# Feed-forward products of a two-layer decode step: five TensorE products for a weight block instead of six

## The chip, the cores and the metric

The kernel runs on one NeuronCore of a Trainium2 chip. The metric is the device time of one execution in microseconds (us). TensorE (PE in the rows) multiplies, with PEld for its weight loads; VectorE (DVE), ScalarE (ACT), GpSimd (POOL) and SyncE (SP) work beside it, each through its own instruction list, in order.

## The reference

Two layers over 512 prompt tokens and 8 sample tokens (T = 520 columns), model width 1024. Layer 0 mixes with an mLSTM, layer 1 with sliding-window attention. Each layer then runs the feed-forward part that this change touches, and a gated per-layer embedding:

```
u = xn @ w_up                              # 1024 -> 2 x 2816
c = conv_b + sum_j up[:, j:j+T] * conv_w[j]  # 3 taps along the tokens
h = silu(c[..., :2816]) * c[..., 2816:]
y = h @ w_down                             # 2816 -> 1024
```

All products are wanted in nearly full float32 precision.

## The kernel before, in words

Features lie on the 128 partitions and tokens along the free axis. Every operand x is split in two float32r parts, high and low (`xH`, `xL`; `hidH`, `hidL`; `wH`, `wL`), and a product is xH·wH + xL·wH + xH·wL, added up in PSUM. A result has 520 columns, more than the 512 of a PSUM bank, so that each of the three is made for two halves of 260 tokens: six products (`product`, L1173) for a weight block of 128 x 128, each with its own weight load.

The work goes by chunks, and a chunk is 128 output rows. In stage `up0` or `up1` there are 44 chunks of 8 weight blocks (48 products), even ones for the gate side and odd ones for the value side. In `down0` or `down1` there are 8 output tiles of two chunks with 11 blocks each (66 products); the last tile is done by halves in another function (`half_product`) and does not change. The first three up chunks (`SPLIT = 3`) also go by halves and do not change.

Two PSUM tiles of two banks each take the results of successive chunks in turn. Chunk c may begin when the tile of chunk c-2 has been read (`free_after`) and when its low weights are ready (`weights_ready`, the semaphore `s_low`).

In the up stages the other engines work on chunk c in this order, each engine's list written out by hand:

- SP loads the raw weights of chunk c+2 when chunk c-1 is done.
- ACT makes the high weights of chunk c+2 (`high`, L756). Then, for an odd c, it applies Silu to the gate side of c-1 (L971), which has to wait until DVE has ended the convolution of c-1 (L2270). For an even c it does a tiny copy (`touch`, L962) and the high half of the hidden tile (`hid_high`, L963), which has to wait for DVE's gating product of c-1 (L2276). Last of all comes the first tap of the convolution (L977), which waits for DVE's read of c.
- DVE waits for the chunk, reads the PSUM tile and scales it by the norm (`scaled_read`, L1880), makes the low weights of chunk c+2 (`low`, L1832), and does the rest of the convolution (L2262, L2264, L2265, L2270). For an even c the low half of the hidden tile of the pair before (L2280) is among it, for an odd c the gating product (L2276) ends it.

In the down stages a hidden tile has to be whole, high and low, before its block is used: the second chunk of the first output tile waits for the last of the 22 (`s_hid`). ACT copies the result out (L990) and squares it (L993), and DVE adds the squares (L2302).

Of the kernel before, what the change touches and what calls it, by code (L numbers as in the profile page):

```python
# [13 lines left out]
P = 128  # L14
# [4 lines left out]
HT = T // 2  # L19
NL = 2  # L20
# [9 lines left out]
FT = 22  # L30
# [32 lines left out]
for _s in ORDER:  # L63
    CHUNK0[_s] = _c
    for _k in range(COUNT[_s]):
# [13 lines left out]
        _c += 1  # L79

# [57 lines left out]
def build(nc, g):  # L138
    with ExitStack() as ctx:
# [29 lines left out]
        xH = sb("xH", [P, KT, T], F32R)  # L169
        xL_at = sb.top  # L170
        xL = sb("xL", [P, KT, T], F32R)
# [35 lines left out]
        eye = const[:, C_EYE:C_EYE + DEC * DEC]  # L207
        low_at = sb.top
        gate_more = at("gate_more", [P, 2, T], sb.top)
        sg = [u[:, r, 2:2 + T] for r in range(2)] + [gate_more[:, r, :] for r in range(2)]  # L210
        pH = sb("pH", [P, EKT, T], F32R)
        pin_at = sb.top
        pL = sb("pL", [P, EKT, T], F32R)
        pin = at("pin", [P, EKT, T], pin_at)
        arena = sb.top
# [4 lines left out]
        hidH = ff("hidH", [P, FT, T], F32R)  # L220
        hidL = ff("hidL", [P, FT, T], F32R)
# [6 lines left out]
        pxH = em("pxH", [P, KT, T], F32R)  # L228
        pxL = em("pxL", [P, KT, T], F32R)
# [122 lines left out]
        s_psq = sem("ple_square")  # L352
        s_out, s_ystored = sem("stored"), sem("y_stored")
# [48 lines left out]
        def depth(c):  # L402

            return next(DEPTHK[s] for s in reversed(ORDER) if CHUNK0[s] <= c)

# [88 lines left out]
        def _(sp):  # L494
# [54 lines left out]
        def band_and_sinks(pool):  # L549
            made = Chain(pool, s_made)  # L550
            pool.wait_ge(s_const_rest, 16)
# [69 lines left out]
        def _(pool):  # L621
# [81 lines left out]
            for layer in range(NL):  # L703
# [22 lines left out]
                if layer == 0:  # L726
                    pool.wait_ge(s_mm, CHUNK0["ple0"] + 1 + NEXTRA)
# [20 lines left out]
        def _(act):  # L748
# [31 lines left out]
            def inputs(stage, k, q, layer, norm):  # L780
# [4 lines left out]
                nc.scalar.activation(square(stage, q, k), h[:, k, tokens(q)], ACT.Square).then_inc(s_sq, 1)  # L785

# [54 lines left out]
            for c in range(COUNT["kv"]):  # L841
# [11 lines left out]
                if c == 8:  # L853
                    act.wait_ge(s_dml, 1)
                    nc.scalar.activation(wcol[:], wcol[:], ACT.Exp).then_inc(s_wcol, 1)
            def outer_product(b):
# [37 lines left out]
            for c in range(COUNT["qo"]):  # L894
# [7 lines left out]
                if c == 11:  # L902
                    sigmoids(4, 7)

# [11 lines left out]
            def feed_forward(layer, mixer, y, beside):  # L916
# [48 lines left out]
                for c in range(UP):  # L965
# [15 lines left out]
                for c in range(COUNT[down] - 2):  # L981
# [4 lines left out]
                    if c % 2:  # L986
                        k = c // 2
                        act.wait_ge(s_mm, CHUNK0[down] + c + 1)
                        src = bank(down, k)[:, :, 0:HT]
                        nc.scalar.activation(halves(y_down[:, k, :]), src, ACT.Copy)  # L990
                        if k >= 2:
                            act.wait_ge(s_acc, ACC0[down] + k)
                        nc.scalar.activation(halves(sq[:, k % 2, :]), src, ACT.Square).then_inc(s_yr, 1)  # L993
# [52 lines left out]
                def sigmoid(c):  # L1046

                    act.wait_ge(s_read, READ0[ple] + c + 1)
# [93 lines left out]
            for c in range(COUNT["qkv"]):  # L1142
# [8 lines left out]
                if 2 <= c < LASTQ:  # L1151
                    rotate(c)
                if c == 0:
                    act.wait_ge(s_ss, SUM["qkv", 0])
                    nc.scalar.activation(halves(rstd[:]), sums[:, :, 0:HT], ACT.Sqrt, bias=eps[:, 0:1],
                                         scale=1.0 / D).then_inc(s_root, 1)
            exps(BESIDE)
# [14 lines left out]
        def _(pe):  # L1172
            def product(c, w, x, k, out, first, last):  # L1173

                wh, wl = (t[SLOT[c]][:, w * P:w * P + P] for t in (wH, wL))
                for q in range(2):
                    nc.tensor.matmul(out[:, q, 0:HT], wh, x[0][:, k, tokens(q)], start=first, stop=False)  # L1177
                for q in range(2):
                    nc.tensor.matmul(out[:, q, 0:HT], wh, x[1][:, k, tokens(q)], start=False, stop=False)  # L1179
                for q in range(2):  # L1180
                    mm = nc.tensor.matmul(out[:, q, 0:HT], wl, x[0][:, k, tokens(q)], start=False, stop=last)  # L1181
                return mm

            def half_product(c, w, x, k, q, out, first, last):

                wh, wl = (t[SLOT[c]][:, w * P:w * P + P] for t in (wH, wL))
                nc.tensor.matmul(out, wh, x[0][:, k, tokens(q)], start=first, stop=False)  # L1187
                nc.tensor.matmul(out, wh, x[1][:, k, tokens(q)], start=False, stop=False)  # L1188
                return nc.tensor.matmul(out, wl, x[0][:, k, tokens(q)], start=False, stop=last)  # L1189
# [4 lines left out]
            def chunk(stage, k0, x, fresh=False, between=lambda k: None):  # L1194
# [4 lines left out]
                for k in range(KT):  # L1199
                    if fresh:  # L1200
                        pe.wait_ge(s_xr, XSET[stage] + k + 1)
                    mm = product(c, k, x, k, out, k == 0, k == KT - 1)
# [54 lines left out]
            X = (xH, xL)  # L1257
# [43 lines left out]
            def first_chunk(c, k0, k1):  # L1301

                for k in range(k0, k1):
                    if c == 0:
                        pe.wait_ge(s_xr, k + 1)
                    mm = product(c, k, X, k, bank("kv", c), k == 0, k == KT - 1)
# [206 lines left out]
            def feed_forward(layer, mixer, beside):  # L1513
# [30 lines left out]
                d0, hid = CHUNK0[down], (hidH, hidL)  # L1544
                for k0 in range(KT - 1):
                    for part in range(2):
# [9 lines left out]
                        for k in range(DKH):  # L1556
                            mm = product(c, k, hid, part * DKH + k, bank(down, k0), k == 0 and part == 0,
                                         k == DKH - 1 and part == 1)
# [19 lines left out]
                for j in range(KT):  # L1578
# [3 lines left out]
                    for q in range(2):  # L1582
                        if j >= 2:
                            pe.wait_ge(s_pwr, 2 * KT * layer + 2 * (j - 2) + q + 1)
                        for k in range(EKT):
                            mm = half_product(c, EKT * jj + k, (pH, pL), k, q, p_bank(j)[:, q, 0:HT], k == 0, k == EKT - 1)
# [159 lines left out]
            def first_chunks():  # L1746

                def tiles(c, k0, k1):
                    for k in range(k0, k1):
                        pe.wait_ge(s_xr, XSET["qkv"] + k + 1)  # L1750
                        mm = product(CHUNK0["qkv"] + c, k, (pxH, pxL), k, bank("qkv", c), k == 0, k == KT - 1)
# [18 lines left out]
            for c in range(2, COUNT["qkv"]):  # L1770
# [19 lines left out]
                chunk("qkv", c, (pxH, pxL), between=attend)  # L1790
# [33 lines left out]
        def _(dve):  # L1824
# [52 lines left out]
            def scaled_read(stage, c, dst, rows=P, scale=1.0):  # L1877

                dve.wait_ge(s_mm, CHUNK0[stage] + c + 1)
                nc.vector.scalar_tensor_tensor(out=halves(dst), in0=bank(stage, c)[0:rows, :, 0:HT], scalar=scale,  # L1880
                                               in1=halves(rstd[0:rows, :]), op0=ALU.mult, op1=ALU.mult
# [885 lines left out]
```

## Time and profile before

| | us |
|---|---|
| median of 3 runs (1296.8 to 1296.97) | 1296.81 |
| span of the profiled execution | 1294.8 |
| PE busy in it | 1287.4 |
| DVE busy in it | 891.1 |
| ACT busy in it | 594.0 |
| POOL busy in it | 75.0 |

The profiled execution has a span of 1294.8 us, from its first to its last instruction; the timed runs are 2.0 us above that, for what lies around the span. In the rows, L1880 is line 1880 of the kernel before. A timeline row gives the start, the duration, the engine, the line, the operation with the tile written and the tiles read, the shape and the number of instructions merged; in brackets stands idle time before it and what ended it. PEclk is the share of TensorE's full clock (2.4 GHz) that was granted.

### The profile page before, as it was taken

To read this page: it belongs to the slowest core of one execution; us is meant where nothing else is said; L and a number is where in the kernel's file an instruction comes from. 1 tells how busy PE (TensorE), PEld (TensorE's weight loads), DVE (VectorE), ACT (ScalarE), POOL (GpSimd) and SP (SyncE) were. 2 spreads that over 40 slices of the span, in tenths; PEclk is the share of its full clock that TensorE was granted. 3 is DMA by queue.
4 is the path that set the end of the run, shared out by engine and by line. 5 is a ranking of instruction groups with operands and counts; after the bars stand their busy time and mean duration, and the time that the engine had idled before them with its cause. 6 is when DMAs were issued, how large, how long until landed. Compare 5 with 4: busy or idle time off the path is not lost.

```text
span 1294.8 us, 25277 instructions
## 1 busy us (share of the span) xinstructions
PE 1287.4 (99%) x10786; PEld 1254.7 (97%) x10786; DVE 891.1 (69%) x1602; ACT 594.0 (46%) x1060; POOL 75.0 (6%) x117
## 2 busy tenths in 40 slices
PE   9999999999999999999999999999999999999998
PEld 8999989999999999999999978999999999999998
DVE  7899776987777774223897787688777777422385
ACT  6214565544444443223855677554444444222381
POOL 1112230000100000000031020000000000000000
PEclk9999999999999999999999999999999999999999
DMA  5435521213343233222314232311322323322231
GB/s 199 155 100 194 198 99 53 103 58 106 95 105 94 87 111 114 90 90 78 138 59 148 68 97 81 113 52 50 98 94 87 98 84 110 114 90 90 79 130 67
DMA packets 35616, 131.84 MB, mean 102 GB/s; under 512 B 4516, under 2 KB 5260, under 8 KB 35184
## 3 DMA queue, kind: packets, MB, share of 16 engines
q1 hardware_dynamic: 29664, 111.33, 26.8%
q0 software_dynamic: 5408, 18.26, 4.3%
q8 instruction: 85, 1.39, 0.4%
q10 hardware_dynamic: 432, 0.64, 0.2%
q14 instruction: 27, 0.22, 0.1%
HBM read 121.26 MB, written 10.08 MB: 101 GB/s over the span
## 4 chain that ended last, share of the span: by engine, by line
PE 95%; DVE 3%; ACT 1%; DMA 0%; issue 0%; ACTq 0%; DVEq 0%
PE tile L1177 24%; PE tile L1181 24%; PE tile L1179 24%; PE tile L1187 5%; PE tile L1188 5%; PE tile L1189 4%; PE tile L1649 1%; PE side L1187 1%; PE side L1188 1%; PE side L1189 1%; PE sums L1226 0%; DMA raw<-in_w_kv 0%; PE sums L1700 0%; PE sums L1348 0%; PE sums L1707 0%
## 5 line engine op out<-in xcount | busy, mean ns | idle before, releaser
L756 ACT ACTIVATE wH<-raw 128x1024 fp32r<-128x1024 f32 (+1 forms) x190 | 210.9, 1113 | 377.4 <-DMA raw<-in_w_up 145.9
L1177 PE MATMUL tile<-xH,wH 128*128 128x260 f32 x1798 | 362.7, 283 | 0.1
L1181 PE MATMUL tile<-xH,wL 128*128 128x260 f32 x1798 | 362.4, 283 | 0.0
L1179 PE MATMUL tile<-xL,wH 128*128 128x260 f32 x1798 | 361.8, 283 | 0.0
L1832 DVE TENSOR_TENSOR wL<-raw,wH 128x1024 fp32r<-128x1024 f32 (+1 forms) x190 | 245.7, 1294 | 154.5 <-ACT wH L756 150.4
L1177 PEld LDWEIGHTS tile<-xH,wH 128*128 128x128 f32 x1798 | 277.1, 188 | 3.5 <-issue 3.0
L1181 PEld LDWEIGHTS tile<-xH,wL 128*128 128x128 f32 x1798 | 277.2, 188 | 0.0
L1179 PEld LDWEIGHTS tile<-xL,wH 128*128 128x128 f32 x1798 | 276.4, 188 | 0.0
L1880 DVE SCALAR_TENSOR_TENSOR u<-tile,rstd 128x520 f32<-128x520 f32 x96 | 67.2, 700 | 119.5 <-PE tile L1181 119.4
L1177 PE MATMUL tile<-hidH,wH 128*128 128x260 f32 x616 | 124.3, 283 | 0.0
L1181 PE MATMUL tile<-hidH,wL 128*128 128x260 f32 x616 | 123.8, 282 | 0.0
L1179 PE MATMUL tile<-hidL,wH 128*128 128x260 f32 x616 | 123.8, 282 | 0.0
L1187 PE MATMUL tile<-xH,wH 128*128 128x260 f32 x400 | 116.0, 290 | 0.1
L1188 PE MATMUL tile<-xL,wH 128*128 128x260 f32 x400 | 113.1, 283 | 0.0
L1189 PE MATMUL tile<-xH,wL 128*128 128x260 f32 x400 | 112.8, 282 | 0.0
L1179 PEld LDWEIGHTS tile<-hidL,wH 128*128 128x128 f32 x616 | 95.1, 188 | 0.0
L1181 PEld LDWEIGHTS tile<-hidH,wL 128*128 128x128 f32 x616 | 94.9, 188 | 0.0
L1177 PEld LDWEIGHTS tile<-hidH,wH 128*128 128x128 f32 x616 | 94.8, 188 | 0.0
L1187 PEld LDWEIGHTS tile<-xH,wH 128*128 128x128 f32 x400 | 75.3, 188 | 2.8 <-issue 2.3
L1188 PEld LDWEIGHTS tile<-xL,wH 128*128 128x128 f32 x400 | 75.3, 188 | 0.3
L1189 PEld LDWEIGHTS tile<-xH,wL 128*128 128x128 f32 x400 | 75.3, 188 | 0.0
L977 ACT ACTIVATE cv<-u,taps 128x520 f32<-128x520 f32 x44 | 36.2, 824 | 48.2 <-DVE u L1880 47.8
(446 smaller groups left out, 1913.9 us busy)
## 6 DMA issues: line engine op xcount, KB each, us to landing
raw<-in_w_up SPq DMA_DIRECT2D x88, 512.0 KB, 3.6
raw<-in_w_down SPq DMA_DIRECT2D x32, 704.0 KB, 4.1
raw<-in_w_ple SPq DMA_DIRECT2D x16, 512.0 KB, 5.6
raw<-in_w_qo SPq DMA_DIRECT2D x12, 512.0 KB, 3.6
raw<-in_w_qkv SPq DMA_DIRECT2D x12, 512.0 KB, 3.5
raw<-in_w_kv SPq DMA_DIRECT2D x10, 512.0 KB, 3.7
cring<-in_c_in POOLq DMA_DIRECT2D x8, 512.0 KB, 4.8
out_c_s<-cring POOLq DMA_DIRECT2D x8, 512.0 KB, 3.2
```

The lines of the kernel that those rows point to most:

```text
L756: nc.scalar.activation(wH[j][:, 0:n], raw[j][:, 0:n], ACT.Copy).then_inc(s_high, 1)
L977: nc.scalar.activation(dst[:], u[:, r, 2:], ACT.Identity, bias=taps[:, r, 3:4], scale=taps[:, r, 2:3]).then_inc(s_ca, 1)
L1177: nc.tensor.matmul(out[:, q, 0:HT], wh, x[0][:, k, tokens(q)], start=first, stop=False)
L1179: nc.tensor.matmul(out[:, q, 0:HT], wh, x[1][:, k, tokens(q)], start=False, stop=False)
L1181: mm = nc.tensor.matmul(out[:, q, 0:HT], wl, x[0][:, k, tokens(q)], start=False, stop=last)
L1187: nc.tensor.matmul(out, wh, x[0][:, k, tokens(q)], start=first, stop=False)
L1188: nc.tensor.matmul(out, wh, x[1][:, k, tokens(q)], start=False, stop=False)
L1189: return nc.tensor.matmul(out, wl, x[0][:, k, tokens(q)], start=False, stop=last)
L1649: nc.tensor.matmul(banks[half][:, e, at0 + 2 * HD - HD * m + k0:at0 + 3 * HD], queries[r, gp, m * P:m * P + P], qk[r, gp // 2, k0:HD * m + ...
L1832: nc.vector.tensor_tensor(wL[j][:, 0:n], raw[j][:, 0:n], wH[j][:, 0:n].bitcast(F32), ALU.subtract).then_inc(s_low, 1)
L1880: nc.vector.scalar_tensor_tensor(out=halves(dst), in0=bank(stage, c)[0:rows, :, 0:HT], scalar=scale, in1=halves(rstd[0:rows, :]), op0=ALU. ...
```

## The change

For the up chunks from the fourth on and for the down tiles but the last, `wide_product` takes the place of `product`. It splits the tokens in 256 and 264. High and low rows are put beside each other in memory, so that one product of 512 columns makes wH·xH and wH·xL of the first 256 tokens at once, into the two halves of one PSUM bank. wL·xH of those tokens is added to the second half. The other 264 tokens take three products in the second bank, as before.

So the first 256 columns of the result lie in two parts. ACT copies the first part to SBUF (`set_apart`), DVE adds it to the second part in PSUM (`join`), and then 520 columns of the result lie side by side and are read as before. On ACT the copy stands behind Silu or `hid_high` of the same chunk; on DVE the addition stands ahead of the read. The place of the copy in SBUF is that of the constant `band`, which is now loaded on POOL's queue when the last join of layer 0's down stage is done; SP loads the other constants in two pieces, not one.

```diff
+def wide(stage, c):
+    if stage[:2] == "up":
+        return c >= SPLIT
+    return stage[:4] == "down" and c < KT - 1
...
+            def wide_product(c, w, x, k, out, first, last):
+
+                wh, wl = (t[SLOT[c]][:, w * P:w * P + P] for t in (wH, wL))
+                right = out[:, 1, 0:T - WIDE]
+                nc.tensor.matmul(out[:, 0, :], wh, x[:, :, k, 0:WIDE], start=first, stop=last, skip_group_check=True)
+                nc.tensor.matmul(right, wh, x[:, 0, k, WIDE:T], start=first, stop=False)
+                nc.tensor.matmul(right, wh, x[:, 1, k, WIDE:T], start=False, stop=False)
+                nc.tensor.matmul(out[:, 0, WIDE:2 * WIDE], wl, x[:, 0, k, 0:WIDE], start=False, stop=last, skip_group_check=True)
+                return nc.tensor.matmul(right, wl, x[:, 0, k, WIDE:T], start=False, stop=last)
...
+            def set_apart(stage, c):
+                if wide(stage, c):
+                    j = JOIN[stage, c]
+                    act.wait_ge(s_mm, CHUNK0[stage] + (2 * c + 2 if stage[:4] == "down" else c + 1))
+                    if j:
+                        act.wait_ge(s_joined, j)
+                    nc.scalar.activation(apart(stage), bank(stage, c)[:, 0, 0:WIDE], ACT.Copy).then_inc(s_apart, 1)
...
                         hid_high(c // 2 - 1)
+                    set_apart(up, c)
                     act.wait_ge(s_read, READ0[up] + c + 1)
...
+            def join(stage, c):
+                if wide(stage, c):
+                    j, low_results = JOIN[stage, c], bank(stage, c)[:, 0, WIDE:2 * WIDE]
+                    dve.wait_ge(s_apart, j + 1)
+                    nc.vector.tensor_tensor(low_results, low_results, apart(stage), ALU.add).then_inc(s_joined, 1)
...
+                join(stage, c)
                 dve.wait_ge(s_mm, CHUNK0[stage] + c + 1)
+                if wide(stage, c):
+                    dve.wait_ge(s_joined, JOIN[stage, c] + 1)
...
-                        act.wait_ge(s_mm, CHUNK0[down] + c + 1)
-                        src = bank(down, k)[:, :, 0:HT]
+                        set_apart(down, k)
+                        act.wait_ge(s_joined, JOIN[down, k] + 1)
+                        src = results(down, k)
...
                         k = c // 2
+                        join(down, k)
                         dve.wait_ge(s_yr, YREAD0[down] + k + 1)
...
-                        sp.dma_start(const[:, C_CAUSAL:], g.const[:, C_CAUSAL:]).then_inc(s_const_rest, 16)
+                        for piece in (slice(C_CAUSAL, C_BAND), slice(C_SEL, C_ALL)):
+                            sp.dma_start(const[:, piece], g.const[:, piece]).then_inc(s_const_rest, 16)
...
                 if layer == 0:
+                    pool.wait_ge(s_joined, JOIN["down0", KT - 2] + 1)
+                    pool.dma_start(band, g.const[:, C_BAND:C_SEL]).then_inc(s_band, 16)
                     pool.wait_ge(s_mm, CHUNK0["ple0"] + 1 + NEXTRA)
```

## Rows read from the trace of the kernel before

**Rows 1.** The page: span, and the chain of waits by engine.

```profile
span 1294.8 us, 25277 instructions
...
PE 95%; DVE 3%; ACT 1%; DMA 0%; issue 0%; ACTq 0%; DVEq 0%
```

**Rows 2.** Windows (PE, PEld, DVE, ACT, POOL busy; clock; DMA; GB/s): up0, down0, up1.

```profile
256.00:488.00 232.00, 231.96 (x1931) 231.75 (x1930) 172.61 (x331) 101.09 (x144) 5.49 (x5) 1.00 0.32 93
487.00:607.00 120.00, 120.00 (x1000) 120.00 (x1000) 35.82 (x32) 33.32 (x39) 1.10 (x2) 1.00 0.29 96
...
870.00:1102.00 232.00, 231.96 (x1930) 231.75 (x1930) 171.82 (x331) 101.29 (x144) 0.00 (x0) 1.00 0.28 87
```

**Rows 3.** Groups by shape, PEld: one form of weight load (busy us, mean ns).

```profile
L1181 PEld LDWEIGHTS tile<-xH,wL 128*128 128x128 f32 x1798 | 277.2, 188 | 0.0
```

**Rows 4.** Timeline of PE in layer 0's mixer: products of other shapes.

```profile
155.63 1.95 PE L1378 MATMUL tile<-kvq 128*128 128x128 f32 x16
...
172.64 1.03 PE L1400 MATMUL tile<-vtok,prob 128*128 128x257 f32 x4
173.50 0.60 PE L1402 MATMUL tile<-cv,prob 128*128 128x257 f32 x2
```

**Rows 5.** Timeline of DVE, up0: an even chunk, an odd one, the next.

```profile
401.12 0.70 DVE L1880 SCALAR_TENSOR_TENSOR u<-tile,rstd 128x520 f32<-128x520 f32 x1 [1.31 <-PE tile L1181]
401.85 1.22 DVE L1832 TENSOR_TENSOR wL<-raw,wH 128x1024 fp32r<-128x1024 f32 x1
...
404.42 0.74 DVE L2270 SCALAR_TENSOR_TENSOR cg<-u,taps,cg 128x512 f32<-128x512 f32 x1
...
406.88 0.70 DVE L1880 SCALAR_TENSOR_TENSOR u<-tile,rstd 128x520 f32<-128x520 f32 x1 [1.64 <-PE tile L1181]
...
409.70 0.75 DVE L2270 SCALAR_TENSOR_TENSOR cv<-u,taps,cv 128x512 f32<-128x512 f32 x1
410.56 0.70 DVE L2276 TENSOR_TENSOR cv<-cg,cv 128x520 f32<-128x520 f32 x1
...
412.65 0.70 DVE L1880 SCALAR_TENSOR_TENSOR u<-tile,rstd 128x520 f32<-128x520 f32 x1 [1.31 <-PE tile L1181]
```

**Rows 6.** Timeline of ACT in the same chunks.

```profile
405.88 1.06 ACT L756 ACTIVATE wH<-raw 128x1024 fp32r<-128x1024 f32 x1 [3.20 <-DMA raw<-in_w_up]
406.85 0.62 ACT L971 ACTIVATE cg<-cg 128x520 f32<-128x520 f32 x1
```

**Rows 7.** Groups by shape: the nearest kin of copy and addition.

```profile
L801 ACT ACTIVATE y_ml<-tile 128x260 f32<-128x260 f32 x16 | 6.2, 387 | 15.6 <-PE tile L1189 15.5
...
L1888 DVE TENSOR_TENSOR u<-tile,rstd 128x260 f32<-128x260 f32 x8 | 3.1, 423 | 0.1
```

**Rows 8.** Timeline of all engines as chunks 3 and 4 are read.

```profile
261.67 0.69 DVE L1880 SCALAR_TENSOR_TENSOR u<-tile,rstd 128x520 f32<-128x520 f32 x1
261.72 0.64 ACT L971 ACTIVATE cg<-cg 128x520 f32<-128x520 f32 x1 [2.17 <-DVE cg L2270]
...
265.73 0.70 DVE L1880 SCALAR_TENSOR_TENSOR u<-tile,rstd 128x520 f32<-128x520 f32 x1
```

**Rows 9.** Timeline of all engines, chunk 43's read to the second down chunk.

```profile
487.62 0.70 DVE L1880 SCALAR_TENSOR_TENSOR u<-tile,rstd 128x520 f32<-128x520 f32 x1 [1.24 <-PE tile L1181]
488.35 1.62 DVE L1832 TENSOR_TENSOR wL<-raw,wH 128x1408 fp32r<-128x1408 f32 x1
...
491.69 0.70 DVE L2276 TENSOR_TENSOR cv<-cg,cv 128x520 f32<-128x520 f32 x1
492.42 0.20 ACT L962 ACTIVATE touch<-eps 128x1 f32<-128x1 f32 x1 [3.18 <-DVE cv L2276]
492.53 0.62 ACT L963 ACTIVATE hidH<-cv 128x520 fp32r<-128x520 f32 x1
...
493.18 0.70 DVE L2280 TENSOR_TENSOR hidL<-cv,hidH 128x520 fp32r<-128x520 f32 x1 [0.80 <-ACT hidH L963]
...
495.33 0.41 PE L1177 MATMUL tile<-hidH,wH 128*128 128x260 f32 x2
```

More of the change, by code:

```diff
@@ L19 @@
 HT = T // 2
+WIDE = 256
 NL = 2
@@ L79 @@
         _c += 1
+def wide(stage, c):
+    if stage[:2] == "up":
+        return c >= SPLIT
+    return stage[:4] == "down" and c < KT - 1
+JOIN = {}
+for _s in ORDER:
+    for _k in range(KT if _s[:4] == "down" else COUNT[_s]):
+        if wide(_s, _k):
+            JOIN[_s, _k] = len(JOIN)
 READ0, YREAD0, ACC0, SUM, MA0 = {}, {}, {}, {}, {}
@@ L404, in depth, with apart, results, as_results @@
             return next(DEPTHK[s] for s in reversed(ORDER) if CHUNK0[s] <= c)
+        def apart(stage):
+            return apart_late[:] if stage[:3] == "ple" or stage == "qkv" else apart_early
+        def results(stage, c):
+            if wide(stage, c):
+                return bank(stage, c)[:].rearrange("p q t -> p (q t)")[:, WIDE:WIDE + T]
+            return bank(stage, c)[:, :, 0:HT]
+        def as_results(stage, c, ap):
+            return ap if wide(stage, c) else halves(ap)
         def halves(ap):
@@ L1201, in chunk @@
                         pe.wait_ge(s_xr, XSET[stage] + k + 1)
-                    mm = product(c, k, x, k, out, k == 0, k == KT - 1)
+                    mm = (wide_product if wide(stage, k0) else product)(c, k, x, k, out, k == 0, k == KT - 1)
                     if k < KT - 1:
@@ L1305, in first_chunk @@
                         pe.wait_ge(s_xr, k + 1)
-                    mm = product(c, k, X, k, bank("kv", c), k == 0, k == KT - 1)
+                    mm = (wide_product if wide("kv", c) else product)(c, k, X, k, bank("kv", c), k == 0, k == KT - 1)
                 if k1 == KT:
@@ L1542, in feed_forward @@
                     chunk(up, c, X)
-                d0, hid = CHUNK0[down], (hidH, hidL)
+                d0, hid = CHUNK0[down], hidHL
                 for k0 in range(KT - 1):
@@ L1556, in feed_forward @@
                         for k in range(DKH):
-                            mm = product(c, k, hid, part * DKH + k, bank(down, k0), k == 0 and part == 0,
-                                         k == DKH - 1 and part == 1)
+                            mm = wide_product(c, k, hid, part * DKH + k, bank(down, k0), k == 0 and part == 0,
+                                              k == DKH - 1 and part == 1)
                         mm.then_inc(s_mm, 1)
@@ L1750, in tiles @@
                         pe.wait_ge(s_xr, XSET["qkv"] + k + 1)
-                        mm = product(CHUNK0["qkv"] + c, k, (pxH, pxL), k, bank("qkv", c), k == 0, k == KT - 1)
+                        mm = (wide_product if wide("qkv", c) else product)(CHUNK0["qkv"] + c, k, pxHL, k, bank("qkv", c), k == 0, k == KT - 1)
                     if k1 == KT:
@@ L1789, in _ @@
                     pe.wait_ge(s_soft, g)
-                chunk("qkv", c, (pxH, pxL), between=attend)
+                chunk("qkv", c, pxHL, between=attend)
                 if c == 2:
```

63 lines of the change are left out of this document (36 added, 27 removed).

## The prediction, made before the run

> **What bounds the kernel now.** I read the page first: a span of 1294.8 us, and a chain of waits that is PE for 95% of it [rows 1]. Then the windows by stage. In the up stage of layer 0 PE is busy for 231.96 of 232 us with 1931 products, which is 120.1 ns each, at a granted clock of 1.00 (2.4 GHz); in the down stage for 120.00 of 120 us, 1000 products, 120 ns each. Layer 1 repeats layer 0 to the hundredth [rows 2]. DVE is busy for 172.6 of the 232 us and ACT for 101.1. So PE is the bound, and the views that decide are two others: what a product costs apart from its columns, and how long the way is round DVE and ACT from one chunk to the next, because the change adds two steps to that way.
>
> An up chunk is 48 products. Reads of chunks stand at 401.12, 406.88 and 412.65 [rows 5]: 5.765 us a chunk, 11.53 us a pair.
>
> **What PE gains.** At 2.4 GHz 260 columns are 108.3 ns; the product takes 120.1, so 11.8 ns are beside the columns. The block before has 6 x 260 = 1560 columns, the new one 512 + 3 x 264 + 256 = 1560, the same. It has one product less. If the 11.8 ns belong to each product, a block falls from 721 to 709 ns. Bounds, since no float32r product of another width is in the trace: if the excess goes with the columns, the gain is nothing. If instead the weight load paces the products (it is busy for 188 ns at a time, overlapping, and PEld is as full as PE [rows 2, 3]), the four narrow ones stay at 120 ns and the wide one takes its 213.3 ns and 2.5 more. The 2.5 is from a stream of other products: four of 257 columns from 172.64 to 173.50, 215 to 217 ns each, where two passes over 257 columns are 214.2 [rows 4]. That is 696 ns, a gain of 24. A stream with 128 columns and a weight load of the same size goes at about 112 ns ((1.95 - 0.27)/15) [rows 4], so that a load need not take 120 by itself; I take 11.8, between the two.
>
> The row says 120.1 ns for a product of 260 columns. The Trainium skill (TensorE: Matmul & The Clock Gate, Back-to-back issue gap) gives a warm gap of columns / 2.4 + 2.5 ns, which would be 110.8; the trace disagrees. By that rule one product less would save only 2.5 ns a block, and the sum below would end at an estimated 1305.4 us.
>
> Blocks that change: 41 chunks x 8 + 14 x 11 = 482 a layer, 964 in all. If PE set the pace everywhere, the gain would be 964 x 11.8 ns = 11.4 us.
>
> **What the copy and the addition cost.** Nearest kin: an ACT copy of 260 columns from PSUM takes 387 ns, a DVE product of two operands, one in PSUM, 423 ns [rows 7]. For 256 columns I take 0.385 and 0.42 us. DVE's target is PSUM here, which no row shows; at worst I take 0.48, at best 0.38, and for the copy 0.35 to 0.45. Neither step can go into idle time as such, because they lie in a ring. I follow it through, with R for the start of a read and S for the start of the addition.
>
> - S to R: 0.42, and 0.10 for a wait on DVE's own last result behind another wait (the gating product starts at 410.56 where L2270 ended at 410.45 [rows 5]): 0.52.
> - R to the end of the convolution, even chunk: 401.12 to 405.16, 4.04 [rows 5]. Then a crossing to ACT (0.03, as from 492.39 to 492.42 [rows 9]), Silu 0.62, an overlap of 0.09 (406.94 against 406.85 [rows 6]), the copy 0.385, a crossing back 0.03. Even S to odd S: 0.52 + 4.04 + 0.975 = 5.535.
> - R to the end of the gating product, odd chunk: 406.88 to 411.26, 4.38 [rows 5]. Crossing 0.03, `touch` 0.11 until the next starts, the high half 0.62 [rows 9], then -0.09 + 0.385 + 0.03. Odd S to even S: 0.52 + 4.38 + 1.085 = 5.985.
>
> The pair takes 11.52 us. PE alone would take 11.53 - 16 x 0.0118 = 11.34. In the kernel before this ring is open: the read waits for PE alone, and Silu and the high half are done beside PE's next chunk, so that DVE is idle 1.3 to 1.6 us ahead of each read [rows 5]. Now the read waits for the copy, the copy stands behind Silu or `hid_high` on ACT, and these wait for DVE's work on the chunk before. Behind the waiting read on DVE stand the low weights of chunk c+2, and PE waits for those. A lag, once there, can't be made up, for the ring is no faster than PE.
>
> And there is a lag from the start. Chunk 3 is read at 261.67, long after it is done, since DVE and ACT are busy with the first chunks. Silu ends at 262.36 [rows 8]. The copy then ends at 262.66, S(3) = 262.69, R(3) = 263.21. From read 3 to read 4 DVE takes 4.06 us (265.73 - 261.67 [rows 8]), so the gating product ends at 267.27, S(4) = 267.27 + 1.085 = 268.36, R(4) = 268.88: 3.15 us later than before. Chunk 5 starts 1.5 us late (it needs read 3), chunk 6 some 2.6 us late (low weights ready at 268.88 + 0.73 + 1.22 = 270.83). S(5) = 268.88 + 4.04 + 0.975 = 273.90. From there 19 pairs to chunk 43: 273.90 + 19 x 11.52 = 492.78, and 0.40 for the longer low weights in chunk 42 (1.62 against 1.22 [rows 5, 9]): 493.18. R(43) = 493.70, where it was 487.62 [rows 9].
>
> The second down chunk needs the last hidden tile. Before, its low half ended at 493.88, 6.26 us behind R(43), covered by the first down chunk, and PE began at 495.33 [rows 9]. Now it ends at 499.96, and PE begins at 499.99: 4.66 us later, 9.3 us for two layers. Note that PE's own speed doesn't enter into this: up to here the ring sets the time.
>
> Behind that point PE is the bound again. In the down stages DVE is busy for 35.8 and ACT for 33.3 of 120 us [rows 2]; copy and addition lie beside 15.9 us for each tile and cost nothing (without that cover 0.8 us a tile). 13 down chunks a layer, 286 blocks in all, gain 286 x 11.8 ns = 3.4 us. The split load of constants is one DMA issue more on SP early in the first stage, and `band` on POOL's queue is small and awaited much later, by the work on POOL that begins in `ple0`: nothing.
>
> Sum: +9.3 - 3.4 = +5.9 us. The profiled span of 1294.8 would be about 1300.7, the median 1296.8 + 5.9 = **1302.7 us**, slower by 0.45%.
>
> **Rivals.**
> 1. The weight load sets the pace. The ring part stays, down gains 286 x 24 ns = 6.9: +2.4, 1299.2 us. For it speaks that PEld is as full as PE; against it the stream at 112 ns.
> 2. One product less gains next to nothing (the excess goes with the columns): +9.3, 1306.1 us. The rule of the Trainium skill that is cited above would come out near it, at 1305.4 us.
> 3. The other sign: the ring is shorter than I count, and the lag fades. It decides when a pair of chunks takes less than 11.34 us, that is 0.18 less than my sum, 0.09 for each copy and addition, or if Silu and `hid_high` wait less than counted. Then PE is the bound from about chunk 7 on, the two layers lose 2 x 2.6 us at the start and gain 916 x 11.8 ns = 10.8: -5.6, 1291.2 us. For it: each term is small and taken from a neighbour. Against it: all but the addition are seen in this very loop.
> 4. The product of 512 columns, with rows in two runs, goes at half pace, like the 257 columns in 217 ns: a block of some 905 ns, 964 x 184 ns = 177 us more, 1474 us. Nothing speaks for it.
>
> **How the numbers follow.** Chances: forecast 0.50, rival 1 0.20, rival 2 0.15, rival 3 0.12, rival 4 0.03. An error of 0.01 us a chunk in the ring is 39 x 2 x 0.01 = 0.8 us; with copy and addition at their ends (-0.07 and +0.12 a chunk) the sum moves by -5.5 and +9.4, of which I take less than half as likely, 2.5 either way. The range goes from rival 1 less 2.5 to rival 2 and 2.5 more, rounded: 1297 to 1309 us. Within 0.2% (1294.2 to 1299.4 us, what a measurement of this kernel can tell from no change) lies half of rival 1 and little else: 0.13. Slower 0.75, faster 0.12.
>
> **What would show it.** In the profile after: PE idle at chunks 5 and 6, then short waits on the low weights (L1832's successor) every second chunk, the reads spaced by 11.5 us a pair as before; each addition on DVE waiting for ACT, not for PE; a wait of about 2 us for the last hidden tile at the second down chunk; down chunks of 7.80 us where 66 products took 7.93. Wrong at the ring if the reads are spaced by 11.34 or less; wrong at PE if down chunks stay at 7.93 or fall to 7.67.

## The result, and the profile after

The changed kernel takes 1308.17 us (median; 1307.92 to 1308.55), the kernel before in the same session 1296.8 us: a ratio of 1.0089 with an interval of 1.0074 to 1.0103, 11.4 us slower. The forecast was 1302.7, or 5.9 us slower. Its profiled execution spans 1306.3 us against 1294.8 [rows 1], 11.5 us more, at a granted clock of 1.00 in both, so the two profiles can be set against each other.

The page of the kernel after: span, chain of waits by engine, and the group of the new addition.

```profile
span 1306.3 us, 23679 instructions
...
PE 57%; DVE 33%; ACT 6%; issue 4%; DMA 0%; DVEq 0%; ACTq 0%
...
L1943 DVE TENSOR_TENSOR tile<-tile,const 128x256 f32<-128x256 f32 x96 | 42.4, 442 | 95.6 <-ACT const L830 95.6
```

PE is still busy for 99% of the span, but the chain that ended last runs over PE for 57% of it and no longer for 95% [rows 1]; for 39% it goes through DVE and ACT. That is the sign of a ring: PE looks busy, and what sets the time is the way round two other engines. The last row says where: ahead of the 96 additions DVE was idle for 95.6 us, all of it until ACT's copy (L830), none until PE.

The windows of `up0` and `down0` (columns as in [rows 2]):

```profile
255.00:487.00 232.00, 228.75 (x1580) 213.57 (x1579) 185.24 (x360) 109.09 (x179) 5.49 (x5) 1.00 0.30 90
503.00:603.00 100.00, 100.00 (x701) 93.81 (x700) 29.27 (x27) 27.84 (x32) 0.25 (x1) 1.00 0.29 97
```

In the up stage PE is idle for 3.3 us, where it was for 0.04 [rows 2]; in the down stage, from 503 us on, it is never idle. Of the 3.3 us, 2.6 lie where the forecast had them, ahead of chunks 5 and 6; the rest is waits for low weights at two late rounds, which it did not have. The waits are longer than this idle time: a product is shown as busy for 0.28 us though the next starts 0.12 us later, so that a wait of less than 0.16 us does not appear at all. All engines as chunk 3 is copied, added and read:

```profile
261.82 0.64 ACT L1018 ACTIVATE cg<-cg 128x520 f32<-128x520 f32 x1 [2.17 <-DVE cg L2341]
...
262.15 0.28 PE L1232 MATMUL tile<-xHL,wL 128*128 128x264 f32 x1
262.37 0.37 ACT L830 ACTIVATE const<-tile 128x256 f32<-128x256 f32 x1
262.76 0.43 DVE L1943 TENSOR_TENSOR tile<-tile,const 128x256 f32<-128x256 f32 x1 [0.90 <-ACT const L830]
263.31 0.70 DVE L1951 SCALAR_TENSOR_TENSOR u<-tile,rstd 128x520 f32<-128x520 f32 x1
...
264.06 0.51 PE L1228 MATMUL tile<-xHL,wH 128*128 128x512 f32 x1 [1.63 <-DVE u L1951]
```

Silu, then the copy, then the addition (262.76; forecast 262.69), then the read (263.31; forecast 263.21), then PE, which had issued its last product at 262.15 and starts chunk 5 at 264.06, a gap of 1.91 us (1.63 of it counted as idle). From there the rounds on DVE repeat:

```profile
273.95 0.43 DVE L1943 TENSOR_TENSOR tile<-tile,const 128x256 f32<-128x256 f32 x1 [0.90 <-ACT const L830]
274.50 0.70 DVE L1951 SCALAR_TENSOR_TENSOR u<-tile,rstd 128x520 f32<-128x520 f32 x1
...
279.94 0.43 DVE L1943 TENSOR_TENSOR tile<-tile,const 128x256 f32<-128x256 f32 x1 [0.99 <-ACT const L830]
280.48 0.70 DVE L1951 SCALAR_TENSOR_TENSOR u<-tile,rstd 128x520 f32<-128x520 f32 x1
...
285.51 0.43 DVE L1943 TENSOR_TENSOR tile<-tile,const 128x256 f32<-128x256 f32 x1 [0.90 <-ACT const L830]
286.05 0.70 DVE L1951 SCALAR_TENSOR_TENSOR u<-tile,rstd 128x520 f32<-128x520 f32 x1
```

Reads follow each other by 5.98 and 5.57 us, 11.55 a pair (forecast 11.52; PE's own 11.53 in the kernel before [rows 5], and 11.51 with five products, as the first experiment below shows). The lag of the first chunks is never made up. At the end of the up stage DVE reads chunk 43:

```profile
495.04 0.43 DVE L1943 TENSOR_TENSOR tile<-tile,const 128x256 f32<-128x256 f32 x1 [0.90 <-ACT const L830]
495.59 0.70 DVE L1951 SCALAR_TENSOR_TENSOR u<-tile,rstd 128x520 f32<-128x520 f32 x1
```

and PE from the end of the first down chunk to the second, which needs the last hidden tile:

```profile
499.94 0.28 PE L1232 MATMUL tile<-hidHL,wL 128*128 128x264 f32 x1
501.90 0.50 PE L1228 MATMUL tile<-hidHL,wH 128*128 128x512 f32 x1 [1.68 <-DVE hidHL L2351]
```

501.90 instead of 495.33 [rows 9]: 6.57 us lost in layer 0, where 4.66 was forecast. At the same point of layer 1 PE is 11.21 us behind the kernel before.

### The profile page after: what moved, and what is told of

It is laid out like the page before. It is cut to its first block, busy times and chain, and to the rows that moved or that the text cites. A ratio compares the mean times of both kernels' runs of the same rounds, so it can differ in the third digit from the quotient of the medians.

```text
span 1306.3 us, 23679 instructions
## 1 busy us (share of the span) xinstructions
PE 1288.3 (99%) x9822; PEld 1210.5 (93%) x9822; DVE 934.3 (72%) x1698; ACT 621.9 (48%) x1156; POOL 75.5 (6%) x118
## 4 chain that ended last, share of the span: by engine, by line
PE 57%; DVE 33%; ACT 6%; issue 4%; DMA 0%; DVEq 0%; ACTq 0%
DVE wL L1893 8%; PE tile L1238 6%; PE tile L1242 6%; PE tile L1240 6%; PE tile L1228 5%; DVE u L1951 5%; PE tile L1248 4%; PE tile L1249 4%; PE tile L1250 4%; DVE tile L1943 3%; PE tile L1229 3%; PE tile L1232 3%; PE tile L1230 3%; PE tile L1231 3%; DVE cv L2341 3%
## 5 line engine op out<-in xcount | busy, mean ns | idle before, releaser
L1228 PE MATMUL tile<-xHL,wH 128*128 128x512 f32 x656 | 261.6, 399 | 5.8 <-DVE u L1951 3.3
L1232 PE MATMUL tile<-xHL,wL 128*128 128x264 f32 x656 | 186.7, 285 | 0.0
L1229 PE MATMUL tile<-xHL,wH 128*128 128x264 f32 x656 | 186.7, 285 | 0.0
L1230 PE MATMUL tile<-xHL,wH 128*128 128x264 f32 x656 | 186.5, 284 | 0.0
L1231 PE MATMUL tile<-xHL,wL 128*128 128x256 f32 x656 | 185.1, 282 | 0.0
L1230 PEld LDWEIGHTS tile<-xHL,wH 128*128 128x128 f32 x656 | 123.2, 188 | 29.5
L1228 PEld LDWEIGHTS tile<-xHL,wH 128*128 128x128 f32 x656 | 123.5, 188 | 7.3 <-DVE u L1951 3.7
L1228 PE MATMUL tile<-hidHL,wH 128*128 128x512 f32 x308 | 122.1, 396 | 3.7 <-DVE hidHL L2351 3.4
L1232 PEld LDWEIGHTS tile<-xHL,wL 128*128 128x128 f32 x656 | 123.5, 188 | 0.0
L1229 PEld LDWEIGHTS tile<-xHL,wH 128*128 128x128 f32 x656 | 123.4, 188 | 0.0
L1231 PEld LDWEIGHTS tile<-xHL,wL 128*128 128x128 f32 x656 | 123.3, 188 | 0.0
L1248 PE MATMUL tile<-xHL,wH 128*128 128x260 f32 x400 | 116.0, 290 | 0.1
L1249 PE MATMUL tile<-xHL,wH 128*128 128x260 f32 x400 | 113.1, 283 | 0.0
L1250 PE MATMUL tile<-xHL,wL 128*128 128x260 f32 x400 | 112.8, 282 | 0.0
L1943 DVE TENSOR_TENSOR tile<-tile,const 128x256 f32<-128x256 f32 x96 | 42.4, 442 | 95.6 <-ACT const L830 95.6
L1238 PE MATMUL tile<-xHL,wH 128*128 128x260 f32 x486 | 98.6, 284 | 0.0
L1242 PE MATMUL tile<-xHL,wL 128*128 128x260 f32 x486 | 97.9, 283 | 0.0
L1240 PE MATMUL tile<-xHL,wH 128*128 128x260 f32 x486 | 97.8, 283 | 0.0
L1232 PE MATMUL tile<-hidHL,wL 128*128 128x264 f32 x308 | 87.7, 285 | 0.0
```

The source lines that it names most:

```text
L1228: nc.tensor.matmul(out[:, 0, :], wh, x[:, :, k, 0:WIDE], start=first, stop=last, skip_group_check=True)
L1229: nc.tensor.matmul(right, wh, x[:, 0, k, WIDE:T], start=first, stop=False)
L1230: nc.tensor.matmul(right, wh, x[:, 1, k, WIDE:T], start=False, stop=False)
L1231: nc.tensor.matmul(out[:, 0, WIDE:2 * WIDE], wl, x[:, 0, k, 0:WIDE], start=False, stop=last, skip_group_check=True)
L1232: return nc.tensor.matmul(right, wl, x[:, 0, k, WIDE:T], start=False, stop=last)
L1238: nc.tensor.matmul(out[:, q, 0:HT], wh, x[:, 0, k, tokens(q)], start=first, stop=False)
```

## The experiments

Every kernel was timed against the kernel before, which stood at 1296.5 us (1296.8 in the session of the result). The diffs are against the changed kernel and are shown in part.

**Five products without the ring, and the ring without five products.** The first leaves out copy and addition and all waits on them; the product of the high weights and the high rows of the first 256 tokens is still made, but is missing from the results:

```
 def set_apart(stage, c):
-    if wide(stage, c):
+    if False:
 def join(stage, c):
-    if wide(stage, c):
+    if False:
```

> Five products, the wide one among them, but no copy and no addition: the first 256 tokens lack the part wH x xH, which this kernel leaves out of its results. Theory (ring): PE is the bound, blocks of 716 ns: 1296.8 - 4.5 = 1292.3 us. If the weight load set the pace, 1296.8 - 23 = 1274 us; if each product had 11.8 ns beside its columns, 1285.4. Rival (the wide product is to blame for the loss): about 1308 us.

Measured: 1294.47 us, ratio 0.9984 (0.9975 to 0.9994), 2.2 us above the 1292.3 that were expected. An up chunk takes 5.753 us against 5.766 before, 11.51 a pair: an up block gains 1.5 ns and not the 4.7 counted on.

The second keeps copy and addition in their places, though the sum goes into columns that nobody reads, and goes back to six narrow products:

```
+for weights, row, start, stop in ((wh, 0, first, False), (wh, 1, False, False), (wl, 0, False, last)):
+    for dst, columns in parts:          # 256 and 264 columns
+        mm = nc.tensor.matmul(dst, weights, x[:, row, k, columns], start=start, stop=stop)
```

> Six narrow products (256 and 264 columns) as before, but the copy and the addition are still made, in the same places, into columns that nobody reads. Theory (ring): the up stages are set by the ring whatever PE does, so that only the gain in the down stages goes: 1308.2 + 1.3 = 1309.5 us, with reads 11.56 us a pair as in the changed kernel. Rival (the wide product is slow or waits): without it the time comes back to about 1297 us.

Measured: 1309.13 us, ratio 1.0097 (1.0080 to 1.0114), with the reads again by 5.57 and 5.98 us.

So the six products of before with the two new steps are as slow as the change, and the five products without them are 2.0 us faster than before. The five products are worth little, and copy and addition, with the waits that they bring, cost 13.7 us (1308.17 - 1294.47; 13.4 if each is taken against the kernel before of its own session).

**Is it the work of the two steps, or their place in the order?** Same work, other order: on ACT the copy ahead of Silu and the high half of the hidden tile.

```
+                    set_apart(up, c)
                     if r:
                         act.wait_ge(s_cc, UP * layer + c)
                         nc.scalar.activation(cg[:], cg[:], ACT.Silu).then_inc(s_silu, 1)
...
-                    set_apart(up, c)
```

> Theory (ring): the copy stands behind Silu or the high half of the hidden tile on ACT, which wait for DVE's work on the chunk before; with the copy ahead of both, it waits for PE alone and the ring is open. Then PE is the bound with blocks of 716 ns, as in the down stages of the changed kernel, against 721: 964 x 4.7 ns = 4.5 us less than 1296.8, and about 0.5 us a layer more where chunk 3 is read late: 1293.3 us. In the profile an addition that waits for PE's end and 0.4 us, reads 11.46 us a pair. Rival (amount): DVE and ACT simply have too much work with copy and addition, or the wide product is to blame; then the order changes nothing: 1308 us.

Measured: 1296.74 us, ratio 1.0002 (0.9993 to 1.0012). Expected was 1293.3; the 11.4 us of the change are gone, but the faster PE that the expectation still counted on is not there. PE's gap at chunk 5 is 0.92 us in each layer (0.37 in the five products without copy and addition), which is 1.1 of the 2.3 us above 1294.47; another 0.7 lie behind the last product, where this kernel and three others, the changed kernel among them, take 4.9 us and the rest take 4.2. Why they do is not known.

On DVE the low weights of chunk c+2 ahead of the addition and the read of chunk c:

```
+                    if c > SPLIT:
+                        low(*ahead(up, c + 2))
                     read_up(c)
                     if c == 0:
                         low(up, 4)
                         low(up, 5)
-                    if c > SPLIT:
-                        low(*ahead(up, c + 2))
                     conv(c)
```

> DVE makes the low weights of chunk c+2 before it waits for the copy of chunk c, not behind the read. Theory (ring): this takes the 1.22 us of the low weights out of the ring, the pair of chunks could go round in about 9.1 us, and PE no longer waits for low weights that stand behind a waiting read. What is left is the late read of chunk 3, 1.5 us a layer: 1292.3 + 3.0 = 1295.3 us. Rival (amount): nothing changes, 1308 us.

Measured: 1298.03 us, ratio 1.0011 (1.0002 to 1.0021). DVE in its up stage:

```profile
283.75 1.22 DVE L1893 TENSOR_TENSOR wL<-raw,wH 128x1024 fp32r<-128x1024 f32 x1
...
284.96 0.43 DVE L1943 TENSOR_TENSOR tile<-tile,const 128x256 f32<-128x256 f32 x1
285.50 0.70 DVE L1951 SCALAR_TENSOR_TENSOR u<-tile,rstd 128x520 f32<-128x520 f32 x1
```

That is 2.7 us above the 1295.3 that were expected. The low weights now fill the time in which DVE waited for ACT: the addition has no idle time ahead of it. A pair takes 11.03 us until the lag is made up. What is left of the loss is the gap at chunk 5, 1.92 us in each layer as in the changed kernel (0.37 in the five products without copy and addition): 2 x 1.55 = 3.1 of the 3.6 us above 1294.47.

Each of the two orders alone takes away 10.1 or 11.4 us of 13.7, with the same instructions on the same engines. That rules out the work itself, or contention for PSUM or a port, as the main cause. Both together:

> All five products, copy and addition of the change; on ACT the copy stands ahead of Silu and the high half, on DVE the low weights stand ahead of the addition and the read. Theory (the loss lies only in the order of these steps): both openings together leave next to nothing of the ring, the time is that of five products without copy and addition, 1294.5, and at most 1 us for the first chunks: 1294.5 to 1295.5 us, ratio 0.9985 to 0.9992; chunk 5 no longer waits, and an up chunk takes 5.755 us. Rival (copy and addition also cost by contention, for PSUM or for a port, whatever their order): the up chunk stays above 5.765 us and the time is 1296.5 or more, as with one of the two orders alone.

Measured: 1296.19 us, ratio 0.9998 (0.9989 to 1.0006), 0.7 us above what was expected and, within the spread of the runs, no better than the copy first alone. The gap at chunk 5 is 0.91 us in each layer: 1.1 of the 1.7 us above 1294.47. Some 0.3 more lie outside the span, which is 1293.9 us in the median against 1292.45: the timed runs are 2.3 us above it here and 2.0 there. The rest is not explained.

**The change in the down stages alone.**

```
 def wide(stage, c):
     if stage[:2] == "up":
-        return c >= SPLIT
+        return False
```

> The change in the down stages and every stage's wide products but not in the up chunks, which stay at six products with no copy and no addition. Theory (the ring of the up chunks is the whole loss, and one product less is worth about 5 ns a block in the down stages, 1.4 ns in the up stages): no lag, the second down chunk of layer 0 begins within 0.3 us of 495.33, the 286 blocks give 286 x 5 ns = 1.4 us: about 1295.1 us, ratio 0.999. If a block gained the 11.8 ns of the forecast: 1293.1. Rival (copy and addition cost their own time in the down stages too, 0.8 us a tile, 14 tiles): 1306. Rival (the sleepy stretches are caused by the new layout of the activations, not by the ring): over 1299.

Measured: 1295.17 us, ratio 0.9990 (0.9981 to 0.9999). Copy and addition cost nothing that is seen where 15.8 us of PE's work cover each pair of them, and the 286 blocks give 1.3 us: 4.6 ns a block.

**What a product costs beside its columns.** Two kernels without copy and addition. In one the first product has 256 columns and leaves out the high rows:

```
-nc.tensor.matmul(out[:, 0, :], wh, x[:, :, k, 0:WIDE], start=first, stop=last, ...)
+nc.tensor.matmul(out[:, 0, WIDE:2 * WIDE], wh, x[:, 1, k, 0:WIDE], start=first, stop=False, ...)
```

> Five products a block, no copy and no addition, and the first product 256 columns (the low rows of the first 256 tokens) where the change has 512; left out is the product of the high weights with the high rows of the first 256 tokens. It measures what 256 columns more cost in one product. If what lies beside the columns grows with them (about 0.444 ns a column at a granted clock of 1.00): a block falls from 719.4 by 113.7 to 605.7 ns, an up chunk takes 4.846 us, and the time is 1294.5 - 964 x 0.1137 = about 1185 us. If each product has its own fixed 11.8 ns beside columns at 1/2.4 ns: a block falls by 106.7 ns to 612.7, an up chunk takes 4.90 us, and the time is about 1191.7 us. Where DVE's way becomes the bound instead (it is busy for 4.3 us a chunk), the up chunks stay above both and the down chunks decide: 11 blocks 6.66 or 6.74 us.

In the other it has 512 columns of the high rows in one run of memory (x[:, 0, k, 0:2 * WIDE]), in place of 256 high and 256 low ones in two.

> Five products a block, no copy and no addition, and the first product takes 512 columns of the high rows that lie in one run, not 256 of the high and 256 of the low rows in two runs; the results of the first 256 tokens are so wrong in part. If two runs cost something (a restart of the read of the moving rows), the block falls below 719.4 ns: 5 ns a block would be 4.8 us, 1289.7. If the cost goes with the columns alone: within 0.3 us of the kernel with two runs, 1294.2 to 1294.8 us, an up chunk at 5.755 us.

Measured: 1189.31 us and 1293.40 us. Both lie between the two times that were expected. Of the first, an up chunk takes 4.83 us, a little under the lower one, but PE also waits now and then (1.75 us from 280 to 430, in one long round of DVE), so that the blocks decide and not the sum. ACT copies each down tile once, so the spacing of these copies is the time of 22 blocks. Their groups (count, duration ns min/median/max, first and last start), first of the kernel before, then of five products without copy and addition, of the one run, and of the first product with 256 columns:

```profile
L990 ACT ACTIVATE y_down<-tile x7: 604/606/608, 503.5 to 598.7; 128x520 f32<-128x520 f32 x7
```

```profile
L1039 ACT ACTIVATE y_down<-tile x7: 604/606/607, 503.0 to 597.5; 128x520 f32<-128x520 f32 x7
```

```profile
L1039 ACT ACTIVATE y_down<-tile x7: 604/605/608, 502.9 to 597.1; 128x520 f32<-128x520 f32 x7
```

```profile
L1039 ACT ACTIVATE y_down<-tile x7: 603/606/607, 466.9 to 546.3; 128x520 f32<-128x520 f32 x7
```

(598.7 - 503.5) / 6 / 22 gives 721 ns a block before, 716 with the change's five products, 714 with one run, 601.5 with 256 columns less (each good to about 1 ns, since the starts are to 0.1 us; starts read to 0.01 us give 721.2, 716.2, 713.3 and 601.5). 256 columns more in one product therefore cost some 112 ns, 0.44 ns each and not 1/2.4 = 0.417; one product less gives 721.2 - 713.3 = 8 ns; and two runs instead of one cost 3 ns of it. These blocks alone would also fit narrow products that the weight load holds at 120 ns each, whatever their columns, beside one of 233. The starts within the down stage of the kernel with 256 columns less speak against it: the next product starts 118 ns after one of 256 columns and 122 ns after one of 264 (means of over 130 each), so the narrow products go by their columns. In the up chunks the same reads off worse: five products take 5.753 us a chunk (719 ns a block) against 5.766 (721), with one run or two, so that only 1.5 ns a block are gained. Why the up stage gives less than the down stage is open.

**Where the lag comes from.** The lag is how far the reads stand behind those of a kernel that PE alone paces. With the wide chunks beginning at chunk 6 (`return c >= 6` in `wide`) and the order of the change, then with that and the copy first:

> The change as it is (its own order on ACT and DVE), but the up chunks 2 to 5 stay at six products with no copy and no addition; the wide chunks begin at 6. It tells how much of the loss is the lag of the first chunks and how much the closed ring by itself. Theory (a closed ring of 11.55 us a pair against PE's 11.51 loses little by itself; the loss comes from the lag with which it begins): no wait at chunks 5 and 6; read 6 falls at about 275.8, 1.5 us behind PE, the lag grows by 0.04 us a pair, and the second down chunk waits about 0.9 us, 2.1 in layer 0 if a stretched DVE instruction falls there: 1294.5 + 0.9 to 2.1 + 0.9 = 1296.5 to 1297.6 us. Rival (the ring as such costs, wherever it begins): the lag builds up again from chunk 6 and the time is 1304 us or more.

> The up chunks 2 to 5 stay at six products, and from chunk 6 on the copy stands ahead of Silu and the high half on ACT. Theory: neither the lag of the first chunks (0.55 us a layer with the copy first) nor the ring is left, and the time is that of five products without copy and addition: 1294.5 to 1295.1 us, ratio 0.9985 to 0.9990. Rival (copy and addition cost something beside the ring): 1296 us or more.

Measured: 1299.87 us (ratio 1.0026, 1.0016 to 1.0036) and 1294.41 us (0.9986, 0.9977 to 0.9995). The second is as expected and is the fastest kernel of this study with nothing left out: 0.1 us from the five products without copy and addition, 2.1 us under the kernel before and 13.8 under the change. Its ACT, in the up stage:

```profile
280.10 0.38 ACT L830 ACTIVATE const<-tile 128x256 f32<-128x256 f32 x1 [1.18 <-PE tile L1232]
280.38 0.63 ACT L1019 ACTIVATE cg<-cg 128x520 f32<-128x520 f32 x1
...
285.86 0.38 ACT L830 ACTIVATE const<-tile 128x256 f32<-128x256 f32 x1 [1.29 <-PE tile L1232]
```

The copy is released by PE's last product, and Silu stands behind it: the ring is open.

The first kernel misses its 1296.5 to 1297.6 by 2.3 us. Read 6 falls at 275.82 as expected, and the gaps are 5.57 and 5.98, but for four: 8.03 and 6.33 in layer 0, 6.24 and 6.33 in layer 1. The largest, behind ACT:

```profile
357.37 0.82 ACT L1025 ACTIVATE cg<-u,taps 128x520 f32<-128x520 f32 x1 [1.31 <-DVE u L1951]
362.22 1.06 ACT L792 ACTIVATE wH<-raw 128x1024 fp32r<-128x1024 f32 x1 [4.03 <-DMA raw<-in_w_up]
363.19 0.62 ACT L1018 ACTIVATE cg<-cg 128x520 f32<-128x520 f32 x1
363.72 0.36 ACT L830 ACTIVATE const<-tile 128x256 f32<-128x256 f32 x1
```

and on DVE:

```profile
360.60 0.16 DVE L2326 TENSOR_SCALAR taps<-convw 128x4 f32<-128x4 f32 x1
364.11 0.43 DVE L1943 TENSOR_TENSOR tile<-tile,const 128x256 f32<-128x256 f32 x1 [3.35 <-ACT const L830]
```

ACT waits 4.03 us for a weight block; Silu and the copy are queued behind it, DVE waits 3.35 us for the copy, and the round is 2.46 us too long. With the ring closed, nothing takes that up. From 349.39 to 352.83 POOL issues its one transfer of 352 KB (out_conv_old<-in_conv_prev). The kernel before waits for the same block still longer, 5.76 us where 2.0 are usual, and PE does not notice:

```profile
362.31 1.06 ACT L756 ACTIVATE wH<-raw 128x1024 fp32r<-128x1024 f32 x1 [5.76 <-DMA raw<-in_w_up]
```

The changed kernel has a stretched round (6.45 for 5.57) beside the same transfer, here on DVE:

```profile
353.75 2.05 DVE L2326 TENSOR_SCALAR taps<-convw 128x4 f32<-128x4 f32 x1
354.81 1.32 DVE L1943 TENSOR_TENSOR tile<-tile,const 128x256 f32<-128x256 f32 x1
```

and on POOL:

```profile
352.39 3.44 POOL L753 DMA_DIRECT2D out_conv_old<-in_conv_prev  x1 [22.63 <-PE tile L1232]
```

An instruction of 0.16 us takes 2.05 and ends at 355.80, 0.03 us before POOL is done with issuing (355.83). Both kernels with this transfer in the down stage:

```
-pool.wait_ge(s_mm, CHUNK0["up0"] + 4 * len(COPIES) + 4)
-pool.dma_start(g.conv_old, g.conv_prev[:, :, :, 1, :]).then_inc(s_out, 16)
...
 pool.dma_start(pin[:], g.p[layer]).then_inc(s_p, 16)
 if layer == 0:
+    pool.wait_ge(s_mm, CHUNK0["down0"] + 4)
+    pool.dma_start(g.conv_old, g.conv_prev[:, :, :, 1, :]).then_inc(s_out, 16)
```

> The change as it is, but the 352 KB transfer out_conv_old<-in_conv_prev, which POOL issues once in the middle of up0, is issued in down0. It tells what the one stretched round of the ring in layer 0 comes from. Theory (this transfer stretches DVE's instructions and makes a weight block late, and the closed ring hands that on to PE): all gaps between reads in up0 are 5.57 and 5.98 us but for those of the late weights, at least 0.87 us of 1.22 goes, and the time is 1308.2 - 0.9 to 1.2 = 1307.0 to 1307.3 us. Rival (the stretch comes from something else): 1308.2, with a gap of 6.45 us in the same place.

> Wide up chunks from 6 on in the order of the change, and the 352 KB transfer out_conv_old<-in_conv_prev issued in down0. In the kernel with the transfer in up0 one gap between reads was 8.03 us instead of 5.57, behind 4.03 us in which ACT waited for a weight block, and the time 1299.9. Theory (the transfer is the cause): the gap of 8.03 is 5.57, 2.46 us go: 1297.4 us. What is left above 1294.5 is the lag of 1.5 us that the ring keeps and the smaller late weights. Rival (the stretch comes from something else): 1299.9.

Measured: 1307.35 us and 1297.38 us (ratios 1.0089, 1.0075 to 1.0102, and 1.0008, 0.9999 to 1.0017), 0.8 and 2.5 us less than with the transfer in the up stage. Two of the five executions of the first took 1308.65 and 1308.98, so that its times alone would not show the 0.8. The profiles do: the gaps of 6.45 and 8.03 are 5.57; those of 6.33 (and 6.20 in layer 1) stay. The transfer is the cause of the large ones. The one of 6.33 in the changed kernel is not a late weight, but a wait of DVE between its own addition and its read, 0.46 us instead of 0.11, whose cause is open:

```profile
385.67 0.70 DVE L1951 SCALAR_TENSOR_TENSOR u<-tile,rstd 128x520 f32<-128x520 f32 x1 [0.46 <-DVE tile L1943]
```

With the transfer out of the way in both, the wide chunks from 6 on instead of from 3 on are worth 10.0 us (1307.35 - 1297.38), with the ring closed in both: that is, nearly all, the lag of the first chunks.

## Why the prediction was right in its sign and short in its size

The loss was 11.5 us between the profiles where 5.9 were forecast. Of the 5.6 us between them the ring makes 2.6 (11.9 for 9.3), PE's gain 2.1 (1.3 for 3.4), and 0.9 are not explained.

- **What bounds.** Right: the two added steps close a ring over ACT and DVE, and the time up to the second down chunk is set by it, not by PE's speed. Six products or five in it: 1309.13 and 1308.17 us.
- **The ring, step by step.** Copy 0.36 to 0.37 us (taken 0.385), addition 0.43 (0.42), addition to read 0.54 to 0.55 (0.52), even to odd 5.57 (5.535), odd to even 5.98 (5.985), gaps of PE at chunks 5 and 6 of 1.91 and 1.27 us. The 0.03 us a pair too little make 0.6 us over 19 pairs, 1.1 in both layers.
- **R(43).** Forecast 493.70, measured 495.59: 0.6 of the 1.9 us from the line above, 1.2 us from two longer rounds in layer 0 (0.88 and 0.35), and 0.1 from the first and last steps. The forecast left no room for rounds that are late for a reason of their own. The 0.88 are the transfer on POOL (0.8 us by experiment). Its effect was in the kernel before as well, where reads came 6.34 and then 5.19 us apart and a slack of 1.3 to 1.6 us ahead of each read hid it from PE. The 0.35 are not settled.
- **What PE gains.** This is the one term that was mis-sized by itself. 11.8 ns a block were taken between 0 and 24, with the excess of a product as a fixed price. It is 5 ns in the down stages and 1.5 in the up stages: in the down stages about 8 of the 11.8 ns are fixed, two runs take 3 back, and the rest goes with the columns at 0.43 to 0.44 ns each. A down chunk takes 11 x 716 ns = 7.88 us, between the 7.80 of the forecast and the 7.93 of before, and nearer to the latter. The down term is so 1.3 us and not 3.4: 2.1 us of the miss.
- **The sum.** Forecast +5.9. With the measured pieces: 6.57 - 0.65 (down, layer 0) + 5.29 (up and first down chunk of layer 1: 11.21 - 5.92) - 0.65 = +10.6. The profile has +11.5; of the 0.9 that are left, 0.2 arise before the last product and 0.7 in the last stores, and these are not explained.
- **The rivals.** Rival 1 (weight load as the pace) is out at its price, 696 ns a block: the block takes 716, since the product of 512 columns takes some 233 ns from its start to the next, and not 216. Nor does the load hold the narrow products at one pace, by the 118 and 122 ns above. Rival 2 (next to nothing from one product less) was the nearest, at 1306.1, with the ring as forecast. Rival 3 (a shorter ring) didn't happen, but the copy first shows its mechanism: once the ring is open, the lag fades. Its 10.8 us for PE could not have been had. Rival 4 is out by the same 233 ns.
- **The range.** 1308.17 us lies 0.8 under its upper end, which was rival 2 and 2.5 us more for a longer copy and addition. PE's gain was nearly that of rival 2. The ring did take 2.6 us more, but the copy and the addition were as long as taken, so that the range held in part by luck.
- **What was costed at nothing.** Copy and addition in the down stages and the split load of the constants: down only gives 1295.17 us, as the gain of the products alone would.

Where the gain went that five products for six might have brought: there was 2.0 us of it in all, and the order of two queues turned it into a loss of 11.4.

The Trainium skill (TensorE: Matmul & The Clock Gate, Back-to-back issue gap) gives a warm gap of columns / 2.4 + 2.5 ns for a single, isolated product, and says that a stream of weight loads and products goes by other figures. The stream of float32r products in the down stages does not keep to the formula: the fixed part is about 8 ns, and a column costs 0.43 to 0.44 ns.

## What to carry to other kernels

Two steps of 0.4 us each cost 13.7 us here, or next to nothing, by what stood ahead of them in their in-order queues and by the chunk with which they began: before adding a step between PE and its reader, write out the ring engine by engine and compare it with PE's own pace, and put the step ahead of the work that waits for the other engine. A ring as long as PE's own pace isn't neutral: it keeps every lag, that of the first chunks and that of each late block. Start such a change where the slack is there (here from chunk 6) and time one product less on its own before counting on it.

## What the runs showed of the hardware that was not expected

- By the blocks of the down stages, a product of float32r costs 0.43 to 0.44 ns a column at a granted clock of 1.00, with some 8 ns beside them. A moving operand in two runs of 256 columns costs 3 ns more than 512 in one run, in the down stages; in the up stages nothing.
- While POOL issues the transfer of 352 KB (3.44 us), an instruction on DVE can be held up to the end of the issue: 0.16 us became 2.05 (ends 355.80 and 355.83). Not all are: two DVE instructions inside the same 3.44 us took their usual time. In each of the twelve kernels that issue it in the up stage the first instruction held is a TENSOR_SCALAR, and those queued behind it end late with it, while TENSOR_TENSOR and SCALAR_TENSOR_TENSOR that start before it take their usual time. One TENSOR_SCALAR was not held, in the kernel with the low weights first: it started 0.02 us after the issue did and took its 0.16 us. The Trainium skill (SBUF — State Buffer, SBUF: two separate sides) tells of an exclusive lock that GpSimd shares with DVE instructions in a 2-port mode, among others, and that the one which starts first keeps for its whole instruction; the ends agree with that here, but no run shows the lock itself, or the mode of these instructions.
- The same transfer made a weight block late. ACT waited 5.76 us for it in the kernel before (2.0 are usual), 5.18 with five products and no copy and addition, 4.03 with wide chunks from 6 on in the order of the change, and 0.77 in the changed kernel. With the ring closed the wait of 4.03 made a round 2.46 us too long; in the kernel before PE never waited for it.

Two instructions of DVE beside the transfer in the kernel before, where POOL issues from 349.48 to 352.92; the second would usually take 0.17 us:

```profile
349.95 1.23 DVE L1832 TENSOR_TENSOR wL<-raw,wH 128x1024 fp32r<-128x1024 f32 x1
351.10 1.80 DVE L2262 TENSOR_SCALAR newrows<-u 128x10 f32<-128x10 f32 x1
```
